# Rows turned by TensorE go to ScalarE first, compressed scores stand between gate products, sample keys are turned earlier, and the warm-up products are regrouped

## The reference

```python
def compress(kv, pe, w1, w2):      # ch: chunks of 16 rows; a block is two neighbouring chunks
    blocks = jnp.concatenate([ch[:, :-1], ch[:, 1:]], axis=2) + pe[:, None, :]
    hid = jax.nn.gelu(jnp.einsum('bnlhd,lde->bnhe', blocks, w1))
    return jnp.einsum('bnhe,ed->bnhd', hid, w2)

def cmp_attn(q, kc, vc, q_pos, table):
    s = jnp.einsum('bqhgd,bnhd->bqhgn', q, kc).astype(jnp.float32) + bias
    p = masked_softmax(s, (dist >= 0)[:, None, None, :])
    return jnp.einsum('bqhgn,bnhd->bqhgd', p.astype(vc.dtype), vc), p

merged = jax.nn.sigmoid(g_a) * (o_nsa @ prm['w_up_a']) + jax.nn.sigmoid(g_b) * (o_m @ prm['w_up_b'])
```

## Time and profile before

| | us |
|---|---|
| Median of three runs (1686.57 to 1691.50) | 1688.98 |
| The profiled execution's own time | 1690.24 |
| Its span | 1688.6 |
| PE busy in the span | 1634.8 |
| DVE busy | 1115.1 |
| ACT busy | 844.3 |

### The profile page before, as it was taken

How to read it: one execution, slowest core, us unless ns; L and a number is a source line. 1 busy time by engine, 2 the same in 40 slices (tenths; PEclk the granted TensorE clock), 3 DMA queues, 4 the chain that set the end, 5 groups by cost and what they waited for, 6 DMA issues and landing times.

```text
span 1688.6 us, 23899 instructions
## 1 busy us (share of the span) xinstructions
PE 1634.8 (97%) x8908; PEld 1338.0 (79%) x8908; DVE 1115.1 (66%) x1329; ACT 844.3 (50%) x909; POOL 196.4 (12%) x242
## 2 busy tenths in 40 slices
PE   9999999999999999999998999999999999999996
PEld 7877676799999887777666888888888888888874
DVE  4554427366563464443727888888888888888887
ACT  3343422143343233442124677777767767777764
POOL 4321023100000423003204000000000000000020
PEclk9999999999999998999999999999999999999998
DMA  9649161835452865235285999999999999999992
GB/s 279 183 147 292 54 158 43 267 108 157 152 186 88 224 204 149 79 99 124 81 276 197 369 360 404 354 391 358 391 355 396 377 367 405 348 402 350 393 378 105
DMA packets 217988, 424.43 MB, mean 251 GB/s; under 512 B 18006, under 2 KB 113782, under 8 KB 217844
## 3 DMA queue, kind: packets, MB, share of 16 engines
q1 hardware_dynamic: 204592, 382.79, 64.6%
q0 software_dynamic: 12896, 40.29, 7.6%
q10 hardware_dynamic: 420, 0.28, 0.1%
HBM read 403.15 MB, written 24.29 MB: 253 GB/s over the span
## 4 chain that ended last, share of the span: by engine, by line
PE 84%; DVE 7%; ACT 2%; DMA 2%; issue 2%; DVEq 1%; SPq 0%; ACTq 0%
PE ps L763 80%; PE ps L767 4%; DMA weights_in<-in_moe_w 2%; DVE arena L1880 2%; DVE weights_low L1880 2%; ACT weights_high L1455 2%; DVE arena L2249 1%; ACT arena L1452 1%; DVEq L2115 1%; DVE arena L2116 0%; DVE arena L2252 0%; DVEq L2516 0%; DVE arena L2624 0%; ACT arena L1455 0%; DVE arena L2043 0%
## 5 line engine op out<-in xcount | busy, mean ns | idle before, releaser
L1880 DVE TENSOR_TENSOR weights_low<-weights_in,weights_high 128x3072 fp32r<-128x3072 f32 (+1 forms) x192 | 589.4, 3089 | 103.6 <-ACT weights_high L1455 102.5
L1455 ACT ACTIVATE weights_high<-weights_in 128x3072 fp32r<-128x3072 f32 (+1 forms) x192 | 489.6, 2560 | 197.3 <-PE ps L763 166.3
L763 PE MATMUL ps<-arena 128*128 128x288 f32 (+20 forms) x2832 | 522.0, 361 | 18.5 <-DVE arena L1880 10.4
L763 PEld LDWEIGHTS ps<-arena 128*128 128x128 f32 (+9 forms) x2832 | 372.9, 170 | 152.6 <-issue 47.4
L763 PE MATMUL ps<-weights_high,item_high 128*128 128x512 f32 x704 | 277.5, 394 | 7.7 <-DVE weights_low L1880 7.5
L763 PE MATMUL ps<-weights_high,item_low 128*128 128x512 f32 x704 | 274.2, 389 | 0.0
L763 PE MATMUL ps<-weights_low,item_high 128*128 128x512 f32 x704 | 274.0, 389 | 0.0
L763 PEld LDWEIGHTS ps<-weights_high,item_high 128*128 128x128 f32 x704 | 132.2, 188 | 36.3 <-DVE weights_low L1880 10.0
L763 PEld LDWEIGHTS ps<-weights_high,item_low 128*128 128x128 f32 x704 | 132.1, 188 | 28.0
L763 PEld LDWEIGHTS ps<-weights_low,item_high 128*128 128x128 f32 x704 | 132.3, 188 | 26.5
L1452 ACT ACTIVATE arena<-arena 128x128 f32<-128x128 f32 (+12 forms) x191 | 75.5, 409 | 139.4 <-DVE arena L1880 93.5
(11 more groups left out here) (210 smaller groups left out, 1850.0 us busy)
## 6 DMA issues: line engine op xcount, KB each, us to landing
weights_in<-in_moe_w SPq DMA_DIRECT2D x192, 768.0 KB, 8.2
weights_in<-in_moe_w SPq DMA_DIRECT2D x48, 1536.0 KB, 9.6
weights_in<-in_moe_w SPq DMA_DIRECT2D x64, 512.0 KB, 5.0
ffn_in<-in_ffn_w SPq DMA_DIRECT2D x30, 1024.0 KB, 7.0
weights_in<-in_moe_w SPq DMA_DIRECT2D x16, 1024.0 KB, 9.0
arena<-in_w_in SPq DMA_DIRECT2D x32, 384.0 KB, 4.1
token_slots<-arena SPq DMA_DIRECT2D x12, 512.0 KB, 7.8
arena<-in_w_out SPq DMA_DIRECT2D x16, 384.0 KB, 3.7
```

Of the source, the lines that this page charges most:

```text
L763: return nc.tensor.matmul(out, lhsT, rhs, start=start, stop=stop)
L1455: return nc.scalar.activation(out, x, ACT.Copy, scale=scale)
L1880: return V.tensor_tensor(out, x, y, op)
```

## The change

The change has four parts. In the compressed rows ScalarE now copies sets 0, 1, 2, 3, 5 and 7 and VectorE sets 4, 6 and 8; ScalarE copies the first four ahead of `Silu`. The waits of TensorE follow that table. Gate tile 0 is cut into its eight products: four stand ahead of the compressed scores, and one behind each group of four scores. `keys_turned(0)` with its waits moves into round 8 of the loop, ahead of `turn(7)`; VectorE waits for the last turn before it copies turned keys. The 12 products of zeros at the start become 8, and one product of zeros with 128 columns follows each of the eight steps of turned rows.

```diff
-        cv_ev, ..., ct_a, ... = ev("mixer_scalar", 19).steps(1, 1, 4, 1, 5, 1, 1, 1, 1, 2, 1)
-        lf_d, ct_d, ... = ev("compress_vector", 19).steps(1, 4, 1, 1, 2, 8, 1, 1)
+        cv_ev, ..., ct_a, ... = ev("mixer_scalar", 20).steps(1, 1, 4, 1, 6, 1, 1, 1, 1, 2, 1)
+        lf_d, ct_d, ... = ev("compress_vector", 18).steps(1, 3, 1, 1, 2, 8, 1, 1)
+        CT_A, CT_D = (0, 1, 2, 3, 5, 7), (4, 6, 8)
...
-            for i in range(12):
+            for i in range(8):
                 mm(ps[:, 0, 0:N], R[:, 0:P], R)
...
                 i.then_inc(xt_pe.sem, 1)
+                mm(ps[:, 0, 0:P], R[:, 0:P], R[:, 0:P])
...
                 for s in range(9):
-                    if s >= 2:
-                        taken = ct_a if s % 2 == 0 else ct_d
-                        pe.wait_ge(taken.sem, taken.at(l, s // 2))
+                    if s - 2 in CT_A:
+                        pe.wait_ge(ct_a.sem, ct_a.at(l, CT_A.index(s - 2) + 1))
+                    elif s >= 2:
+                        pe.wait_ge(ct_d.sem, ct_d.at(l, CT_D.index(s - 2) + 1))
...
+                def gate_piece(k):
+
+                    sem, at, w = in_of("G0", l)
+                    d = GATE_TILES[0][1]
+                    if k == 0:
+                        pe.wait_ge(sem, at)
+                    m = mm(ps[:, 0, 0:N], w[:, k, (d % 2) * P:(d % 2) * P + P], hT[:, k, :], k == 0, k == KD - 1)
+                    if k == KD - 1:
+                        m.then_inc(gt_pe.sem, 1)
+
                 pe.wait_ge(kt_ev.sem, kt_ev.at(l))
-                gate_tile(0, 0)
-
+                for k in range(4):
+                    gate_piece(k)
                 pe.wait_ge(mqk_ev.sem, mqk_ev.at(l))
                 pe.wait_ge(kc_a.sem, kc_a.at(l))
                 for v in range(KVH):
...
                         if v == 1:
                             m.then_inc(cs_pe.sem, 1)
+                        gate_piece(4 + 2 * v + q)
...
                         scores(p)
                         gate_tile(2 + p, 2 + p % 2)
+                    if p == 8:
+                        pe.wait_ge(sw_in.sem, sw_in.at(l, 304))
+                        pe.wait_ge(gt_ev.sem, gt_ev.at(l, 10))
+                        pe.wait_ge(sa_ev.sem, sa_ev.at(l))
+                        keys_turned(0)
                     if 1 <= p < 9:
                         turn(p - 1)
...
-                pe.wait_ge(sw_in.sem, sw_in.at(l, 304))
-                pe.wait_ge(gt_ev.sem, gt_ev.at(l, 10))
-                pe.wait_ge(sa_ev.sem, sa_ev.at(l))
-                keys_turned(0)
                 pe.wait_ge(on_ev.sem, on_ev.at(l, 1))
                 gate_tile(10, 0)
...
-                act.wait_ge(uc_d.sem, uc_d.at(l))
-                fn(ucT[:, :, :], ucT[:, :, :], ACT.Silu).then_inc(uc_a.sem, 1)
-                for s in range(0, 9, 2):
+                def rows_compressed(s):
+
                     act.wait_ge(ct_pe.sem, ct_pe.at(l, s + 1))
                     for v in range(2):
                         dst, x = compressed(s, v)
                         i = copy(dst, x)
                     i.then_inc(ct_a.sem, 1)
+
+                for s in CT_A[0:4]:
+                    rows_compressed(s)
+                act.wait_ge(uc_d.sem, uc_d.at(l))
+                fn(ucT[:, :, :], ucT[:, :, :], ACT.Silu).then_inc(uc_a.sem, 1)
+                for s in CT_A[4:]:
+                    rows_compressed(s)
...
-                for s in range(1, 9, 2):
+                for s in CT_D:
                     dve.wait_ge(ct_pe.sem, ct_pe.at(l, s + 1))
...
                 dve.wait_ge(gsS_in.sem, gsS_in.at(l))
+                dve.wait_ge(t_pe.sem, t_pe.at(l))
                 def keys_turned(t):
```

More of the change, by code:

```diff
@@ L449, in build @@
         xg_ev, q_ev, kv_ev, u_ev, cst_ev, uc_d, if_ev, qz_ev = ev("mixer_vector", 26).steps(8, 4, 6, 4, 1, 1, 1, 1)
-        cv_ev, gs_ev, o_ev, uc_a, ct_a, kt_ev, lf_a, lf_a2, row_a, hid_ev, kc_a = ev("mixer_scalar", 19).steps(
-            1, 1, 4, 1, 5, 1, 1, 1, 1, 2, 1)
-        lf_d, ct_d, lf_d2, row_d, c_ev, mqk_ev, hidr_ev, kc_d = ev("compress_vector", 19).steps(1, 4, 1, 1, 2, 8, 1, 1)
+        cv_ev, gs_ev, o_ev, uc_a, ct_a, kt_ev, lf_a, lf_a2, row_a, hid_ev, kc_a = ev("mixer_scalar", 20).steps(
+            1, 1, 4, 1, 6, 1, 1, 1, 1, 2, 1)
+        lf_d, ct_d, lf_d2, row_d, c_ev, mqk_ev, hidr_ev, kc_d = ev("compress_vector", 18).steps(1, 3, 1, 1, 2, 8, 1, 1)
         dense_h, dense_l = ev("dense_scalar", 16), ev("dense_vector", 16)
@@ L1035, in values, with keys_turned @@
                                 m.then_inc(pv_pe.sem, 1)
+                def keys_turned(t):
+                    for i in range(16):
+                        r, b, g = i // 8, (i // 2) % 4, i % 2
+                        m = tr(ps[:, 2 + i // 4, (i % 4) * P:(i % 4) * P + P], swK[t][:, r, b, g, :])
+                        if i % 4 == 3:
+                            m.then_inc(skt_pe.sem, 1)
                 pe.wait_ge(kc_d.sem, kc_d.at(l))
@@ L1046, in _ @@
                         values(p - 2)
[L1049 to L1055, removed]
                 def sample_scores(t):
```

## The result

The changed kernel takes 1700.87 us, median of four runs (1699.62 to 1702.63), against 1689.56 for the kernel before in its four runs (1686.57 to 1691.50): ratio 1.0073, 95% interval 1.0058 to 1.0089. It is slower by 0.73%, 11.3 us. The prediction was 1689.0 with a range of 1682 to 1695.5: the sign was missed, and the range too. The profiled execution took 1702.63 us, its span 1700.5, against 1688.6 before.

What follows compares the result with a forecast made beforehand. PE, busy 1634.8 of 1688.6 us, was taken as the bound, losing time to waits and half clock. +4.2 - 2.3 + 0 - 1.7 = +0.2 on 1690.24, less 1.26 to the median, gave 1689 us, range 1682 to 1695.5.

Steps and rivals of the forecast that it cites:

- The start, +4.2: Start: fewer early products plus zeros behind turned rows cost +4.2 us, ends -1.0 and +5.9.
- the bad end: Start: clock falls near 10.7 us, so table products, turns and zeros run slow, +5.9 us.
- two cases: Start: clock falls near 10.7 us (+5.9), or at 14.1 us as before (+2.8).
- +2.8 and +5.9: Start: cost in us if the fall comes at 14.1 as before, and if it comes near 10.7.
- The first rival: Start: zeros hold the clock, -1.0 in place of +4.2, total 1684.0 us; chance 0.22.
- The compressed rows, -2.3: Compressed rows, both layers: new copy order gains, less 1.5 us of clock loss in each layer, -2.3 us.
- The replay: Compressed rows, layer 0 at full clock: new order worked through, `cw1` products start at 106.9 instead of 108.90 us.
- the feared falls: Compressed rows: new holes of 0.6 and 1.4 us bring half clock onto sets 7 and 8 and dense products.
- -5.3 and -0.5: Compressed rows: good end if the clock holds, bad end if it falls in the new holes, in us.
- The compressed scores, 0 with +2.5 as the end: Compressed scores: clock falls all the same, later `Exp`, 0 us taken, ends -0.9 and +2.5.
- The sample keys, -1.7: Last pairs: key turns moved ahead of `turn(7)` fill the 0.83 us wait in each layer, -1.7 us.
- The third rival: Whole kernel: clock falls into the new holes, spells lie on dense products, +7.9, total 1696.9 us; chance 0.14.

Runs made afterwards that it cites:

- the run of the hole alone: Kernel before with 8 instead of 12 products of zeros at the start and no zeros behind the turned rows: ratio 1.0004.
- the rows with their own count: Kernel before with only the new compressed rows order, the four copies ahead of `Silu` counted on a step of their own: ratio 0.9997.
- the even spread: Kernel before with only the compressed scores changed, all eight gate products spread, two behind each group of four scores, none ahead: ratio 1.0071.
- the split with `Exp` first: Kernel before with gate tile 0 cut four ahead, four behind the 16 small products kept together, first `Exp` ahead of `Tanh`: ratio 1.0009.

## Why the prediction was wrong, point by point

**The start, +4.2: too small by 2.3 in the trace.** The hole came as worked out (8.28 to 10.42, ended by the table's DMA), the fall at 10.3 where 10.7 was expected, and the queries at 24.16 where 21 to 23.5 was given. Two terms were mis-sized. A step with its zeros takes 1.39 us at half clock, 0.54 more than a step's 0.85, not the 0.43 taken for a product, so eight cost 4.3 instead of 3.4: the bad end would have been +6.8, and 6.7 was measured. And the fall's place was laid to the hole, which the run of the hole alone contradicts: fall at 13.1, queries at 17.44. Timed, the start costs 0.23%, 3.9 us, and the zeros are most of that (0.16%). That this is close to +4.2 is luck: the forecast was a middle between two cases, and in the worse one the hole did the harm. (The middle of its +2.8 and +5.9 is moreover 4.35.) The first rival (zeros hold the clock) is refuted in its trace: 10.2 us at 1.2 GHz with zeros and no hole. One reading of the stretches was wrong too. Before 14.1 us PE did not turn rows for all of 3.4 us: till 11.47 it made the table's products, then turned the norm vectors, and turned rows only from 11.90, for 2.17 us.

**The compressed rows, -2.3: the step that failed.** The replay assumed that "sets 0 and 1 turned by 99.49; ScalarE copies sets 0 to 3 by 101.8; sets 4 and 5 turned by 102.4", each set released by its own copy. I read the waits by their names and not by the count behind them. The full line of `ev("mixer_scalar")` has `uc_a` ahead of `ct_a`, while the copies moved ahead of `Silu`: the contradiction was there to see. What the runs showed in its place: each of the first waits is met one update late, set 5 waits for `Silu`, and `cw1` begins 12.1 and 12.3 us after the first turn instead of 8.5. Timed, the step cost +0.33%, 5.6 us, where -2.3 was predicted: 7.9 us of the 11.9 by which the forecast fell short. With the count put right the replay held to 0.1 us (8.4 against 8.5), and in its three traces the feared falls did not come, so the bounds of -5.3 and -0.5 were those of another kernel than the one that ran. Even for that kernel the -2.3 is not confirmed: timed it is level with before (0.9997, from 2.9 us less to 1.9 more).

**The compressed scores, 0 with +2.5 as the end: wrong in size.** In the profiled execution they cost 4.0 + 0.9 = 4.9; alone and timed 0.19%, 3.2 us. The chain was read rightly (`Exp` behind the last small product, its load right ahead of it). The clock was not: "I expect the fall all the same" took a spell as long as before, but it became 10.2 us in layer 0 (143.4 to 153.7), where before it was 3.4. Gate tile 1 was then at 1.2 GHz for 5.0 of its 6.3 us in layer 0, against 2.9 of 5.4 before.

**The sample keys, -1.7: right in the traces, not shown by timing.** The wait of 0.83 is gone, that of 1.23 kept. From the first scores of 256 columns to the sample scores the run of the keys alone takes 41.2 us in both layers, 42.07 before: 1.7 in all. The total did not show it (0.9999), but its interval (0.9980 to 1.0017) holds -1.7 as well as nothing.

**Sum and chances.** The third rival named 1696.9, with falls in the holes of all parts. It was the right side, for a partly wrong reason: its rows still gained 0.5. With the first copies counted on a step of their own the whole is at 1.0036, some 1695.6, at the upper edge of the range: the count took the time from there to 1700.9.

On the two places where the prediction drew on the Trainium skill. The Trainium skill ("ScalarE: Activation LUTs", section "What ACT_TABLE_LOAD costs") has a drain beside the load. In after `Tanh` ends at 149.35 and the load starts at 149.37; the load ends at 150.65 and `Exp` starts at 150.66. So none is seen here either, on neither side. The Trainium skill ("TensorE: Matmul & The Clock Gate", section "Part 4: PE-mode transpose") would have the turns not count for the clock. The stretch 94.39 to 102.81 above, 42 turns among its 44 records, stayed at 2.4 GHz, and no fall followed it until 131.1. The trace disagrees.

## What to carry to other kernels

When work is moved past a counted update, write out the count: which update each wait is met by, in the new order. A semaphore shared by two steps turned a harmless reorder into waits that were one update late here, and nothing looked wrong but the time; it can let another waiter pass too early as well. Filler products laid between real work are first of all work: here 0.54 us each at half clock, and the clock fell all the same. Before spreading small products between large ones, look at which engine's list waits for the large ones to be complete.

## What the runs showed of the hardware that was not expected

- A hole of 2.11 us on PE ahead of small products and turns cost nothing measurable (1.0004, fall at 13.1 against 14.1, queries at 17.44 against 17.48).
- Once at 1.2 GHz, PE stayed there for 17.0 us while busy all of that time, with turns, zeros of 128 columns and the first query products (10.42 to 27.40), and for 13.7 us with small and full products mixed, 13.58 of them busy. Before, up to 1600 us, no spell was longer than 6.9. In these spells being busy did not bring the clock back.
- The clock falls at different places in different executions: of ten kernels with the start of before, eight had their first fall between 11.8 and 14.1 us; two (the rows with their own count, the even spread) had none there, and their queries began at 15.18 and 15.42 instead of 17.48. In twelve runs the split with `Exp` first took from 1684.24 to 1697.10 us, and its profiled one was the slowest. A gain of 2 us in a single span proves little.
